# A blocked triangular solve: scores over 64 rows on the array's halves, inverse seeded from masked scores by transposes

## The reference

```python
def step(state, inp):
    r_t, w_t, k_t, v_t, kk_t, a_t = inp
    sa = jnp.einsum('bhvk,bhk->bhv', state, kk_t)
    state = (state * w_t[:, :, None, :]
             - sa[..., None] * (kk_t * a_t)[:, :, None, :]
             + v_t[..., None] * k_t[:, :, None, :])
    return state, jnp.einsum('bhvk,bhk->bhv', state, r_t)
```

## Time and profile before

| what | value |
|---|---|
| median of 3 runs | 3400.41 us (3400.37 to 3401.66) |
| profiled execution, span from first to last instruction | 3400.4 us |
| PE busy | 3153.4 us, 93% |
| DVE busy | 2263.1 us, 67% |
| ACT busy | 1486.1 us, 44% |
| chain that ended last | PE 81%, DVE 14%, ACT 3% |

### The profile page before, as it was taken

One profiled execution on the slowest core, in us unless ns is written; L12 is line 12 of the kernel. 1 busy time (PEld: TensorE's weight loads), 2 busy tenths in 40 slices (PEclk: granted clock), 3 DMA queues, 4 the chain that ended last, 5 costly groups with the idle time before them and its releaser, 6 DMA issues.

```text
span 3400.4 us, 56899 instructions
## 1 busy us (share of the span) xinstructions
PE 3153.4 (93%) x24192; PEld 2979.0 (88%) x24192; DVE 2263.1 (67%) x3345; ACT 1486.1 (44%) x2148; POOL 4.2 (0%) x7
## 2 busy tenths in 40 slices
PE   8999699889999999698899989999999999999899
PEld 7999588779999998587799989987999998877899
DVE  6666867756767667777667665575555558886554
ACT  4445343434444445343344444453444445444443
POOL 0000000000000000000000000000000000000000
PEclk9999899989999999899999999988999999998999
DMA  6664121234656653032246635431454443430244
GB/s 229 235 223 164 50 88 75 101 123 186 226 208 241 239 190 126 13 112 75 100 155 230 235 151 185 161 141 44 157 185 161 184 150 148 150 148 1 95 181 147
DMA packets 72493, 510.98 MB, mean 150 GB/s; under 512 B 8176, under 2 KB 8944, under 8 KB 11440
## 3 DMA queue, kind: packets, MB, share of 16 engines
q1 hardware_dynamic: 72240, 507.33, 40.4%
HBM read 506.25 MB, written 1.05 MB: 149 GB/s over the span
## 4 chain that ended last, share of the span: by engine, by line
PE 81%; DVE 14%; ACT 3%; issue 1%; DMA 1%; SPq 0%; DVEq 0%; ACTq 0%
PE linear_banks L1633 21%; PE linear_banks L1634 21%; PE linear_banks L1635 21%; PE solve_banks L1935 2%; PE solve_banks L1945 1%; DVE qk_rstd L1511 1%; DVE split_halves L1064 1%; DVE inverse L1456 1%; PE solve_banks L1697 1%; DVE modulation_sums L1130 1%; PE solve_banks L2064 1%; PE linear_banks L1715 1%; PE linear_banks L1919 1%; PE linear_banks L1920 1%; DVE rstd L1079 1%
## 5 line engine op out<-in xcount | busy, mean ns | idle before, releaser
L1064 DVE TENSOR_TENSOR split_halves<-raw_units,split_halves 128x1024 fp32r<-128x1024 f32 x806 | 977.1, 1224 | 560.7 <-ACT split_halves L728 555.9
L1633 PE MATMUL linear_banks<-h_split,split_halves 128*128 128x256 f32 x4384 | 1267.2, 289 | 66.9 <-DVE h_split L1094 31.9
L1634 PE MATMUL linear_banks<-h_split,split_halves 128*128 128x256 f32 x4384 | 1250.6, 285 | 0.0
L1635 PE MATMUL linear_banks<-h_split,split_halves 128*128 128x256 f32 x4384 | 1250.0, 285 | 0.0
L728 ACT ACTIVATE split_halves<-raw_units 128x1024 fp32r<-128x1024 f32 x806 | 848.6, 1057 | 739.2 <-PE linear_banks L1635 646.8
L1633 PEld LDWEIGHTS linear_banks<-h_split,split_halves 128*128 128x128 f32 x4384 | 852.1, 194 | 80.2 <-issue 69.4
L1634 PEld LDWEIGHTS linear_banks<-h_split,split_halves 128*128 128x128 f32 x4384 | 852.1, 194 | 1.5 <-issue 1.2
L1635 PEld LDWEIGHTS linear_banks<-h_split,split_halves 128*128 128x128 f32 x4384 | 851.4, 194 | 0.0
L1633 PE MATMUL linear_banks<-hidden_split,split_halves 128*128 128x256 f32 x1408 | 399.0, 283 | 0.0
L1635 PE MATMUL linear_banks<-hidden_split,split_halves 128*128 128x256 f32 x1408 | 397.5, 282 | 0.0
L1634 PE MATMUL linear_banks<-hidden_split,split_halves 128*128 128x256 f32 x1408 | 397.2, 282 | 0.0
(11 more groups left out here) (287 smaller groups left out, 3851.1 us busy)
## 6 DMA issues: line engine op xcount, KB each, us to landing
raw_units<-in_stream SPq DMA_DIRECT2D x403, 1024.0 KB, 4.8
raw_units<-in_mod_w SPq DMA_DIRECT2D x72, 1024.0 KB, 5.8
x<-in_x SPq DMA_DIRECT2D x4, 256.0 KB, 5.2
w2a<-in_w2a SPq DMA_DIRECT2D x2, 512.0 KB, 6.8
w_rows<-in_w SPq DMA_DIRECT2D x2, 512.0 KB, 9.0
bs_rows<-in_bs SPq DMA_DIRECT2D x2, 512.0 KB, 9.9
spatial_t<-in_ws_t SPq DMA_DIRECT2D x2, 512.0 KB, 10.6
out<-x SPq DMA_DIRECT2D x4, 256.0 KB, 4.3
```

The costliest lines, as they stand in the source:

```text
L1064: V.tensor_tensor(split[:, n % SPLIT_SLOTS, 1, :], raw[:, item % RAW_SLOTS, (n % 2) * HALF * P:(n % 2 + 1) * HALF * P], split[:, n % SPLIT ...
L1633: M(o, w_hi, a_hi, start=start, stop=False, skip_group_check=skip)
L1634: M(o, w_hi, a_lo, start=False, stop=False, skip_group_check=skip)
L1635: return M(o, w_lo, a_hi, start=False, stop=stop, skip_group_check=skip)
```

## The change

- The scores contract over 64 rows. `beta` and `kappa` have a single copy for both heads, and each matmul takes one head's 64 partitions of both operands. Both heads of a chunk are formed together, at `score0` (chunk 0) and `score2` (chunk 1), in the order beta head 0, beta head 1, kappa head 0, kappa head 1, each head in its own bank. `score1` and `score3` are empty. The DVE masks two banks in a row.
- DVE's scaling of `kappa` and `beta` is one instruction each over 128 partitions instead of two each over 64. The four clears of the zero halves are gone.
- The mask of the scores now has the sign of the first block in it, and ACT's copy of stage `z` no longer changes the sign.
- The start of the inverse is made anew: ACT copies the identity into `q_inv` at `score0`; at `low` DVE copies the width-1 blocks of `scores` into it under a mask, PE waits for that and transposes the four blocks of `q_inv`, and ACT copies them into `t_inv`. Stage `z` of level 0 waits for that copy.
- The masks have a seventh level (width 1), and some tiles move in SBUF.

```diff
@@ ACT, solve
+                    nc.scalar.activation(q_inv[:, b, :, :], wide(ident, 4), ACT.Copy).then_inc(q_cleared[b], 1)
+                elif stage == "low":
+                    bank = wait_filled(act, ("low", l, c))
+                    nc.scalar.activation(t_inv[:, b, :, :], bank.rearrange("p (a t) -> p a t", a=4), ACT.Copy)\
+                        .then_inc(emptied["act"], 1)
                 elif stage[0] == "z":
                     act.wait_ge(z_done[b], 6 * n + int(stage[1]) + 1)
-                    nc.scalar.activation(z_neg[:, b, :, :], four(0), ACT.Copy, scale=-1.0).then_inc(z_ready[b], 1)
+                    nc.scalar.activation(z_neg[:, b, :, :], four(0), ACT.Copy).then_inc(z_ready[b], 1)
@@ DVE, solve
                     for o, t in ((kappa, k_), (beta, a_)):
-                        for hh in range(2):
-                            w = slice(64 * hh, 64 * hh + 64)
-                            V.tensor_tensor(o[w, hh, :, :], in_chunks(t)[w], neg_incl[w], ALU.mult)
+                        V.tensor_tensor(o[:], in_chunks(t), neg_incl, ALU.mult)
...
                 elif stage[:5] == "score":
                     i = int(stage[5])
-                    bank = wait_filled(dve, ("score", l, c, i))
-                    V.tensor_tensor(gbk[b][:, i, :].rearrange("p (a t) -> p a t", a=2),
-                                    bank.rearrange("p (a t) -> p a t", a=2), wide(mask, 2), ALU.mult)\
-                        .then_inc(emptied["dve"], 1)
+                    if i % 2:
+                        return
+                    for hh in range(2):
+                        bank = wait_filled(dve, ("score", l, c, i + hh))
+                        V.tensor_tensor(gbk[b][:, 2 * hh + i // 2, :], bank, mask, ALU.mult)\
+                            .then_inc(emptied["dve"], 1)
                 elif stage == "low":
-                    bank = wait_filled(dve, ("low", l, c))
-                    V.tensor_tensor(t_inv[:, b, :, :], bank.rearrange("p (a t) -> p a t", a=4),
-                                    wide(c_("neg2"), 4), ALU.mult).then_inc(emptied["dve"], 1)
-                    wait_emptied(dve, ("low", l, c))
-                    V.tensor_tensor(t_inv[:, b, :, :], t_inv[:, b, :, :], wide(ident, 4), ALU.add)\
-                        .then_inc(t_ready[b], 1)
-                    link(V.tensor_tensor(q_inv[:, b, :, :], gbk[b][:, :, 0:CH], wide(c_("neg2t"), 4), ALU.mult))
-                    V.tensor_tensor(q_inv[:, b, :, :], q_inv[:, b, :, :], wide(ident, 4), ALU.add)\
+                    dve.wait_ge(q_cleared[b], n + 1)
+                    wait_emptied(dve, ("score", l, c, 3))
+                    V.copy_predicated(q_inv[:, b, :, :], wide(level_masks[:, 1, 0, :], 4), gbk[b][:, :, 0:CH])\
                         .then_inc(q_started[b], 1)
@@ PE, solve
-                    bank = bank_for(("score", l, c, i))
-                    M(bank[:, 0:2 * CH], beta[:, hh, j, :], ar[:, b, j, :], start=True, stop=True)
-                    M(bank[:, 2 * CH:4 * CH], kappa[:, hh, j, :], ar[:, b, j, :], start=True, stop=True)\
-                        .then_inc(lin_filled, 1)
+                    banks = [bank_for(("score", l, c, i + hh)) for hh in range(2)]
+                    for a, t in enumerate((beta, kappa)):
+                        for hh in range(2):
+                            w = slice(64 * hh, 64 * hh + 64)
+                            ins = M(banks[hh][:, 2 * a * CH:2 * (a + 1) * CH], t[w, i // 2, :], ar[w, b, i // 2, :],
+                                    start=True, stop=True)
+                            if a:
+                                ins.then_inc(lin_filled, 1)
                 elif stage == "low":
                     bank = bank_for(("low", l, c))
+                    pe.wait_ge(q_started[b], n + 1)
                     for i in range(4):
-                        ins = M(bank[:, part(i)], ar[:, b, i % 2, 0:CH], beta[:, i // 2, i % 2, :],
-                                start=True, stop=True)
+                        ins = nc.tensor.transpose(bank[:, part(i)], q_inv[:, b, i, :], ident)
                     ins.then_inc(lin_filled, 1)
...
                     s = int(stage[1])
-                    pe.wait_ge(t_ready[b], 6 * n + s + 1)
                     if s:
+                        pe.wait_ge(t_ready[b], 5 * n + s)
                         pe.wait_ge(q_copied[b], 5 * n + s)
+                    else:
+                        wait_emptied(pe, ("low", l, c))
```

More of the change, by code:

```diff
@@ L41 @@
 LEVELS = (2, 4, 8, 16, 32, 64)
+MASK_LEVELS = (1,) + LEVELS
 MOD_UNITS = 72
@@ L63 @@
 _at = 0
-for _name, _n in (("ident", P), ("mean", P), ("head", P), ("tri", 129), ("mask", 2 * P), ("neg2", P), ("neg2t", P), ("one", 1), ("norm_eps", 1), ("ln_eps", 1)):
+for _name, _n in (("ident", P), ("mean", P), ("head", P), ("tri", 129), ("mask", 4 * P), ("one", 1), ("norm_eps", 1), ("ln_eps", 1)):
     CONST[_name] = (_at, _n)
@@ L217, in make_plan @@
                 p.use(("kbt", l, c + 1), "act")
-            if b and b[:5] == "score":
+            if b in ("score0", "score2"):
                 p.use(("score", l, c + 1, int(b[5])), "dve")
+                p.use(("score", l, c + 1, int(b[5]) + 1), "dve")
             elif b == "low":
-                p.use(("low", l, c + 1), "dve")
+                p.use(("low", l, c + 1), "act")
             stage, s = group_norm_at(c, i)
@@ L328, in build_program @@
     const = place("constants", [P, NCONST])
-    level_masks = place("level_masks", [P, 2, len(LEVELS), P], I8)
+    level_masks = place("level_masks", [P, 2, len(MASK_LEVELS), P], I8)
     cols = place("columns", [P, NCOLS])
@@ L345, in build_program @@
     hidden = over("hidden_split", [P, 2, FT, T], 0, F32R)
-    mod_acc = over("modulation_sums", [P, 2, 2 * P], 104.5)
+    mod_acc = over("modulation_sums", [P, 2, 2 * P], 104.25)
     silu = over("silu", [P, 3, T], 62)
@@ L376, in build_program @@
     ar = over("alpha_rho", [P, 2, NCH, 2 * CH], 92)
[L377 to L383, removed]
+    beta = over("beta", [P, NCH, CH], 96)
+    kappa = over("kappa", [P, NCH, CH], 97)
+    kbt = over("kappa_beta_tok", [P, 2, 2, P], 98)
+    kb0 = over("kappa_beta_0", [P, 2, CH], 100)
+    rh = over("rhs", [P, P], 101)
+    nu = over("neg_u", [P, P], 101.5)
+    s0 = over("state", [P, P], 102)
     ya_hi = over("ya_hi", [P, DT, T], 48, F32R)
@@ L389, in build_program @@
     merged = over("merged", [P, DT, T], 32)
-    level_floats = over("level_floats", [P, 2, len(LEVELS), P], 98)
+    level_floats = over("level_floats", [P, 2, len(MASK_LEVELS), P], 89)
     qk = over("qk", [P, GROUPS, 2 * DT, T], 0)
@@ L473, in build_program @@
     q_copied = [signal(f"q_copied_{b}") for b in range(2)]
+    q_cleared = [signal(f"q_cleared_{b}") for b in range(2)]
     q_started = [signal(f"q_started_{b}") for b in range(2)]
@@ L1296, in rwkv @@
                 bonus_of(l, 3)
-                for b in (beta, kappa):
-                    V.memset(b[0:64, 1, :, :], 0.0)
-                    V.memset(b[64:128, 0, :, :], 0.0)
                 link(V.memset(s0[:], 0.0))
@@ L1455, in solve @@
                     if s < 5:
-                        V.copy_predicated(t_inv[:, b, :, :], wide(level_masks[:, 0, s, :], 4), four(1))\
+                        V.copy_predicated(t_inv[:, b, :, :], wide(level_masks[:, 0, s + 1, :], 4), four(1))\
                             .then_inc(t_ready[b], 1)
                     else:
-                        V.copy_predicated(q_inv[:, b, :, :], wide(level_masks[:, 1, s, :], 4), four(1))\
+                        V.copy_predicated(q_inv[:, b, :, :], wide(level_masks[:, 1, s + 1, :], 4), four(1))\
                             .then_inc(q_final[b], 1)
@@ L1910, in solve @@
                     i = int(stage[5])
-                    hh, j = i // 2, i % 2
+                    if i % 2:
+                        return
                     if i == 0:
@@ L1950, in solve @@
                     s = int(stage[1])
-                    pe.wait_ge(t_ready[b], 6 * n + s + 2)
+                    pe.wait_ge(t_ready[b], 5 * n + s + 1)
                     for i in range(4):
@@ L2126, in constants @@
                                - (i[:, None] <= mid)))
[L2127 to L2130, removed]
+    before, upto = i[:, None] < i[None, :], i[:, None] <= i[None, :]
+    put("mask", np.concatenate([-1.0 * before, upto, before, upto], 1))
     put("one", 1.0)
@@ L2133, in constants @@
     put("ln_eps", LN_EPS)
-    levels = np.zeros((P, 2, len(LEVELS), P), np.float32)
-    for s, m in enumerate(LEVELS):
+    levels = np.zeros((P, 2, len(MASK_LEVELS), P), np.float32)
+    for s, m in enumerate(MASK_LEVELS):
         b = (i[:, None] // m % 2 == 1) & (i[None, :] // m == i[:, None] // m - 1)
```

2 lines of the change are left out of this document (removed).

## The result

The changed kernel took 3423.02 us (median of 4: 3415.42, 3416.11, 3429.93, 3430.39) beside 3401.03 us for the kernel before; the ratio is 1.0063, 95% interval 1.0046 to 1.0080. It is slower, as forecast, by 22 us instead of 9. Timed again later (e4) it took 3418.21, ratio 1.0057. Of all ten executions six lie at 3414 to 3418 and four at 3430 to 3431, and that gap has to be explained too: the median of 3423 lies between the two groups, where no execution does. The kernel before spreads as well: its executions beside the experiments go from 3397 to 3407 us. The first profile is of one at 3416.

The account below looks back on a forecast made before the run. PE's instruction list was taken to set the pace in the two solves. 3400.4 us before, plus 0 for the change without the clock, plus 9 for the clock, gave 3409 us; range 3390 to 3424.

Parts of the forecast that it names:

- Halves side by side: Scores on PE: the two heads' half-height matmuls run concurrently, a group of four taking 0.91 + 0.2 us.
- The wait for scaling: Before the first score transposes: PE's wait of 0.88 us after `z3` for DVE's scaling disappears.
- Three new idle places of PE: In a plain iteration: PE idles 1.5 us before `t3` and 1.8 us before the transposes of `low`.
- the walk: Stage-by-stage timing of a plain iteration at traced times: level 0's `z` starts some 0.4 us later than before.
- rival c: Full iterations: PE's saved time is kept, 2.5 us each, giving 3363 us, or 3382 for half; chance 0.13.
- A fall of the clock: Thin stretch in a solve iteration: 3.4 us at 1.2 GHz, costing 1.6 us; expected in 5 of 14.
- rival a: In the solves: the clock holds despite thinner stretches, 3400.4 us, 3394 to 3406; chance 0.32.
- Sum without the clock: Both solves: plain iterations +0.4 or +0.7, group norm ones -0.4, openings -1.0 each, together 0.0 us.
- the release of `low`: At `low`: PE's transposes wait for DVE's two copies, idle 1.8 us, and start at 553.15.
- Openings: Start of each layer's solve: -1.0 us for DVE's shorter scaling, +0.5 for a clock that rises later.
- Falls inside iterations: In the solves' 14 full iterations: the clock falls in 5, at 1.6 us each.
- the term of the clock: Whole kernel: 5 falls at 1.6 us plus 1 for the openings, +9 us.

Follow-up runs that it names:

- e4: The changed kernel with no edit, timed again and profiled in another execution: 3418.21 us, ratio 1.0057.
- e8: The changed kernel with both heads' score matmuls on partitions 0 to 63, so they cannot run side by side: 3439.47 us, ratio 1.0107.
- e3: The changed kernel with DVE's masked copy of the width-1 blocks one step earlier, at `score3`: 3388.61 us, ratio 0.9961.
- e1: The kernel before with only the new start of the inverse, scores and scaling as before: 3423.14 us, ratio 1.0054.
- e6: e3 with matmuls of constants, results unread, in PE's waits of the openings and last iterations: 3370.17 us, ratio 0.9903.
- e7: The kernel before with matmuls of constants in PE's waits of the openings and last iterations: 3387.42 us, ratio 0.9962.
- e2: The changed kernel with matmuls of constants, results unread, in front of three PE waits: 3410.04 us, ratio 1.0023.

## Why the prediction was right, and where it was off

*Right, and shown.* Halves side by side (timeline after; e8 for the price). The wait for scaling gone. Three new idle places of PE, with the stages behind them within 0.2 us of the walk, the one at `low` named as the cause, and e3 shows it by removing that wait from the full iterations. PE's saved time is lost there and not kept (rival c). A fall of the clock costs 1.6 us: measured 1.0 to 1.7. The clock does not hold (rival a), although no gap of PE in a full iteration of the changed kernel's traces is over 1.73 us; the Trainium skill's warning in "Why this matters for your kernels" (TensorE: Matmul & The Clock Gate) of long idle gaps only does not cover e1, whose clock fell behind a wait of 1.7 us.

*Sum without the clock.* From `z3` to `z3` the six iterations of the first layer's trace changed by +0.9, +0.7, -0.2, +0.45, -0.3 and +0.5, where the walk gave +0.7, +0.7, -0.4, +0.4, -0.4 and +0.4. With the second layer and the seventh iterations, and the one fall taken out, that makes about 4 us where the walk's full iterations came to 2.0. The main slip is the release of `low`: PE started 0.17 us later than in the walk (553.32 instead of 553.15).

*Openings, mis-sized.* The forecast gave -1.0 for DVE's shorter scaling and +0.5 for a clock that rises later, each. The start did move from 414.17 to 413.08. But from there to the next tile's transposes 29.0 and 29.9 us passed instead of 27.3 and 26.5, as the clock stayed at 1.2 GHz for 13.7 and 17.1 us (before: 6.8 and 6.8). In both layers about +4 us against -1. e6 shows that the time is the clock's: with the waits filled, 24.7.

*Falls inside iterations.* Forecast 5; 2 in one execution and 8 in the other, some 3 and 11 us. The forecast took the inner iterations of the kernel before to be free of them; e7 shows that their code is not.

*Last iterations, left out.* I costed them at nothing since their list of instructions is unchanged. In the first profile the second layer's took 68.1 us, counted from the last transposes of `score0` (so with the seventh full iteration) to the next projection, 61.2 before: 27.3 us at 1.2 GHz instead of 13.7, and another 3.4 in the seventh iteration. (The second layer's solve of the kernel before ends at 1695.5 us; the 1711 given under "Time and profile before" is wrong.) That is 6.9 us, in e4 2.6 and 5.8. Part of it may follow from the last full iteration ahead of it, which is changed. But the first layer's last iteration, the same code, moved by 0.1 in the first profile and by 2.6 in e4; what decides the place of a fall in unchanged instructions I have not separated.

The terms for the first profile: first layer's start -1.1, openings +1.6 and +3.4, iterations +1.9 and +3.2 (of these 1.0 for a fall), last ones +0.1 and +6.9, parts between and behind the solves -2.1: 13.9 of the 14.0 us by which its span is longer. The last term is a miss too: the rest of the kernel was to keep its times to within 1 us.

*How much of it was luck.* Mechanism and sign were right; the term of the clock was sized at +9. In the first profile the openings, the last iterations and the falls come to about 13 us by the terms above, in e4's to about 24. The openings' and the last iterations' part of that was forecast at +1 and 0. The median of 3423.02 lies 1 us inside the range's upper end of 3424, and it depends on how the four executions fell: two at 3416, two at 3430, the latter outside the range. The forecast's reasons hold; that the median came out inside is in part luck.

## What to carry to other kernels

In a list that an engine works through in order, price a shorter stage by the next instruction in the list that waits for another engine, not by its own saving: here PE's records fell from 30.4 to 28.8 us in a plain iteration that became 0.7 us longer, and moving one DVE copy a step earlier made the same change worth 13 us instead of costing 17 to 22. When a change takes work out of TensorE, look at the granted clock in the stretches that it thins, the unchanged ones behind it included. Where they are thin and the wait cannot be removed, cheap matmuls in it can be worth more than they cost (18 us from e3 to e6).

## What the hardware showed that I had not expected

Two executions of one kernel, on the same chip and with the same instructions, can differ by 16 us (e4: 3414 to 3431). Of the 14.7 us between the two profiled, 10.4 lie in inner iterations that differ by falls of the clock. A useless matmul in a wait is not neutral: e2 added 15 in each full iteration and became 8 us faster than the changed kernel's e4 median, and e7 took 14 us off a kernel whose instructions were otherwise untouched. In every execution a run's time lies 1.7 to 2.2 us above its span (3416.11 over 3414.4, 3388.61 over 3386.5); the prediction took both for equal. The span of 3400.4 before thus belongs to an execution of about 3402.1, 1.7 us above the median that the sum started from.
